# FFN tile pairs as seven half-size products: every other one from the seventh tile on

## What is computed

```python
def conv_ffn(h, w_up, conv_w, conv_b, w_down):
    up = h @ w_up                                    # 1024 -> 2 * 2816
    gate = causal_dwconv(up[..., :FFN_HIDDEN], conv_w, conv_b)   # 3 taps over tokens
    val = up[..., FFN_HIDDEN:]
    return (jax.nn.silu(gate) * val) @ w_down

for i in range(DEPTH):
    ...
    x = x + rms_norm(m, mix_post_g[i])
    f = conv_ffn(rms_norm(x, ffn_pre_g[i]), ffn_w_up[i], ffn_conv_w[i], ffn_conv_b[i], ffn_w_down[i])
    x = x + rms_norm(f, ffn_post_g[i])
```

## Time and profile before

| | us |
|---|---|
| median of three runs | 1339.46 (1339.46 to 1339.63) |
| profiled execution: own time | 1340.12 |
| profiled execution: span | 1338.4 |
| TensorE busy | 1327.8 (99%) |
| VectorE busy | 786.2 (59%) |
| ScalarE busy | 570.9 (43%) |
| chain that ended last: share of TensorE | 98% |

### The profile page before, as it was taken

How to read it: one execution, slowest core, us unless ns; L and a number is a source line. 1 busy time by engine, 2 the same in 40 slices (tenths; PEclk the granted TensorE clock), 3 DMA queues, 4 the chain that set the end, 5 groups by cost and what they waited for, 6 DMA issues and landing times.

```text
span 1338.4 us, 15750 instructions
## 1 busy us (share of the span) xinstructions
PE 1327.8 (99%) x6382; PEld 1109.5 (83%) x6382; DVE 786.2 (59%) x1140; ACT 570.9 (43%) x875; POOL 28.1 (2%) x30
## 2 busy tenths in 40 slices
PE   8999999999999999999999999999999999999998
PEld 6888888888888888888888888888888888888886
DVE  5888888888526666556632265445566666564223
ACT  6766665556315533333331262223554333333112
POOL 1000000000000000000000000000000000000000
PEclk9999999999999999999999999999999999999999
DMA  5533233442331333333343313334233333334331
GB/s 155 158 110 110 80 97 109 125 121 69 128 108 48 95 107 98 95 95 95 95 137 115 95 32 112 102 102 126 63 88 102 95 97 101 102 96 126 97 109 63
DMA packets 181772, 135.68 MB, mean 101 GB/s; under 512 B 5645, under 2 KB 169893, under 8 KB 180677
## 3 DMA queue, kind: packets, MB, share of 16 engines
q1 hardware_dynamic: 181653, 134.62, 33.5%
q10 hardware_dynamic: 48, 0.07, 0.0%
HBM read 132.51 MB, written 2.16 MB: 101 GB/s over the span
## 4 chain that ended last, share of the span: by engine, by line
PE 98%; ACT 1%; DMA 1%; DVE 0%; issue 0%; SPq 0%; DVEq 0%; ACTq 0%
PE bank L863 22%; PE bank L864 22%; PE bank L865 22%; PE bank L926 9%; PE bank L928 9%; PE bank L927 9%; PE bank L1065 1%; PE bank L1075 1%; PE bank L903 1%; PE bank L1055 1%; DMA x_tok<-in_x 1%; PE bank L1048 1%; PE bank L1040 0%; PE bank L1043 0%; PE bank L1001 0%; ACT mask L423 0%
## 5 line engine op out<-in xcount | busy, mean ns | idle before, releaser
L863 PE MATMUL bank<-h_hi,w_hi 128*128 128x512 f32 (+1 forms) x1328 | 509.0, 383 | 0.0
L865 PE MATMUL bank<-h_lo,w_hi 128*128 128x512 f32 (+1 forms) x1328 | 506.7, 382 | 0.0
L864 PE MATMUL bank<-h_hi,w_lo 128*128 128x512 f32 (+1 forms) x1328 | 506.5, 381 | 0.0
L592 DVE TENSOR_TENSOR w_lo<-w_raw,w_hi 128x1024 fp32r<-128x1024 f32 x227 | 285.1, 1258 | 324.2 <-ACT w_hi L362 324.2
L362 ACT ACTIVATE w_hi<-w_raw 128x1024 fp32r<-128x1024 f32 x227 | 237.1, 1051 | 196.3 <-PE bank L928 172.5
L865 PEld LDWEIGHTS bank<-h_lo,w_hi 128*128 128x128 f32 x1328 | 249.5, 188 | 48.2
L863 PEld LDWEIGHTS bank<-h_hi,w_hi 128*128 128x128 f32 x1328 | 249.6, 188 | 48.0
L864 PEld LDWEIGHTS bank<-h_hi,w_lo 128*128 128x128 f32 x1328 | 249.7, 188 | 47.6
L926 PE MATMUL bank<-w_hi,hid_hi 128*128 128x512 f32 x416 | 162.4, 390 | 0.0
L928 PE MATMUL bank<-w_hi,hid_lo 128*128 128x512 f32 x416 | 161.9, 389 | 0.0
L927 PE MATMUL bank<-w_lo,hid_hi 128*128 128x512 f32 x416 | 161.8, 389 | 0.0
(11 more groups left out here) (145 smaller groups left out, 941.7 us busy)
## 6 DMA issues: line engine op xcount, KB each, us to landing
w_raw<-in_ffn_w_up SPq DMA_DIRECT2D x88, 512.0 KB, 3.8
w_raw<-in_ssd_w_in SPq DMA_DIRECT2D x48, 512.0 KB, 3.9
w_raw<-in_ffn_w_down SPq DMA_DIRECT2D x44, 512.0 KB, 3.5
w_raw<-in_sc_w_in SPq DMA_DIRECT2D x24, 512.0 KB, 3.7
acs_b<-acs_dram SPq DMA_DIRECT2D x8, 1024.0 KB, 6.2
w_raw<-in_ssd_w_out SPq DMA_DIRECT2D x16, 512.0 KB, 3.5
w_raw<-in_sc_w_out SPq DMA_DIRECT2D x8, 512.0 KB, 3.6
x_tok<-in_x SPq DMA_DIRECT2D x4, 512.0 KB, 5.4
```

Of the source, the lines that this page charges most:

```text
L592: nc.vector.tensor_tensor(w_lo[slot(u)][:], w_raw[:, u % 2, :], w_hi[slot(u)][:].bitcast(F32), ALU.subtract).then_inc(w_lo_done, 1)
L863: nc.tensor.matmul(dst, wh, xh, start=start, stop=False)
L864: nc.tensor.matmul(dst, wl, xh, start=False, stop=False)
L865: return nc.tensor.matmul(dst, wh, xl, start=False, stop=stop)
```

## The change

In each layer the FFN tiles 0 to 5 stay plain. From tile 6 on, tiles 6, 8, ... 20 (eight per layer, `FAST`) are **pairs**, computed by the Winograd form of Strassen's scheme; tiles 7, 9, ... 21 stay plain (**singles**). For a pair, the gate and val units are the two rows of a 2 x 2 block matrix A whose columns are the halves of the inner 1024. The tokens' halves and the inner halves give B. Four sums of weights (`weight_sums`: S1, S3, S2, S4) and four sums of B (`block_sums`, once per layer) feed seven products (`up_pair`, `block`), each 4 inner tiles x 3 matmuls of 256 columns. Two of them run on top of an earlier product in the same bank. ScalarE copies three results out (`p1`, `p7`, `p6`), and VectorE makes five sums of 256 columns (`early`, `side`'s halves, `pu`, `late`).

Around it:
- High and low parts are now made of A11 A12, S3 S2, S4 A22 and S1 (`aa_`, `ss_`, `sa_`, `s1_` with `high` on ScalarE and `low` on VectorE): three of 1024 elements and one of 512 per pair, in four slots of the same five. `s_two` and `s_one` hold sums.
- Pairs have two raw buffers of their own, `w_raw_b`. A pair's loads wait for `sa_low` of the pair before.
- `hid` keeps float32 hidden tiles, and the norm row is no longer multiplied into val; the post norm gets a changed epsilon instead (`q_up`, one 128x4 operation on ScalarE at the boundaries before the FFNs). `side`'s multiply is gone from plain tiles: `gate_single` reads the bank.
- Hidden high and low parts are made in the down projection, tiles k + 2 ahead, in a ring of ten (`hs_hi`, `hs_lo`; `hid_high`, `hid_low`). Until the last pair is done, eight of the ten places hold the sums of B.
- `project` now waits ahead of token tile 0 for the last pair's sums, and ahead of tile 3 for all 22 hidden tiles (`hid_taken`).

The core of the diff (`aa_low` stands for its three likes; ScalarE's halves mirror it with the copies, each behind a wait for its slot):

```diff
+    PLAIN = 6
+    FP = (FT - PLAIN) // 2
+    FAST = [U_UP[layer] + 2 * (PLAIN + 2 * i) + half for layer in range(DEPTH) for i in range(FP) for half in range(2)]
...
+    READ = {"A11 A12": 2, "S3 S2": 4, "S4 A22": 6, "S1": 7}
...
+            n = FAST.index(u) // 2
+            for part, read in READ.items():
+                USE[n, part] = len(FREED)
+                FREED.append((True, PRODUCTS * n + read))
...
+        else:
+            RAW_FREED.append((True, FAST.index(u) // 2) if u in FAST else (False, nth(older[-1])))
...
-                sp.dma_start(dst.rearrange(view, n=P) if view else dst, src).then_inc(raw_landed[u % 2], 16)
+                if RAW_FREED[u] is not None:
+                    of_pairs, count = RAW_FREED[u]
+                    sp.wait_ge(sa_lo_done if of_pairs else w_lo_done, count)
...
+                for i in range(FP):
+                    n, t, more = FP * layer + i, PLAIN + 2 * i, i + 1 < FP
+                    single = gate_of(n) + 2
+                    split_at[0] = single
+                    act.wait_ge(prod_done, PRODUCTS * n + 1)
+                    if n:
+                        act.wait_ge(summed_up, SUMS * n)
+                    nc.scalar.copy(p1[:], bank[pair_bank(layer, AT_P1)][:, 0:HALF_T]).then_inc(copied, 1)
+                    splits_to(single + 1)
+                    act.wait_ge(prod_done, PRODUCTS * n + 3)
+                    nc.scalar.copy(p7[:], bank[pair_bank(layer, AT_P7)][:, 0:HALF_T]).then_inc(copied, 1)
+                    splits_to(single + 2)
+                    act.wait_ge(prod_done, PRODUCTS * n + 4)
+                    nc.scalar.copy(p6[:], bank[pair_bank(layer, AT_P1)][:, 0:HALF_T]).then_inc(copied, 1)
+                    if more:
+                        aa_high(layer, i + 1)
+                        ss_high(layer, i + 1)
+                        sa_high(layer, i + 1)
+                    else:
+                        splits_to(single + 4)
...
+            def aa_low(layer, i):
+                n, u = FP * layer + i, gate_of(FP * layer + i)
+                at = slot((n, "A11 A12"))
+                dve.wait_ge(aa_hi_done, n + 1)
+                nc.vector.tensor_tensor(w_lo[at][:], raw(u), w_hi[at][:].bitcast(F32), ALU.subtract).then_inc(aa_lo_done, 1)
...
+                dve.wait_ge(copied, COPIES * n + COPY_P6)
+                dve.wait_ge(prod_done, PRODUCTS * (n + 1))
+                nc.vector.tensor_tensor(pu[:], p6[:], bank[pair_bank(layer, AT_P5)][:, 0:HALF_T], ALU.add).then_inc(summed_up, 1)
+                dve.wait_ge(summed_up, SUMS * n + SUM_U)
+                nc.vector.tensor_tensor(late, pu[:], bank[pair_bank(layer, AT_P3)][:, 0:HALF_T], ALU.add).then_inc(summed_up, 1)
+                dve.wait_ge(summed_up, SUMS * n + SUM_C12)
+                whole = cpad[:, CW - 1:CW - 1 + T]
+                nc.vector.tensor_tensor(whole, whole, r_row[:, 0, :], ALU.mult).then_inc(gate_in, 1)
+                nc.vector.tensor_tensor(side[:, HALF_T:], pu[:], p7[:], ALU.add).then_inc(summed_up, 1)
...
+                    whole(b12, 0, 1)
+                elif part == 1:
+                    dve.wait_ge(t_made, at + 2)
+                    nc.vector.tensor_tensor(b11, b12, b11, ALU.subtract).then_inc(t_made, 1)
+                    whole(b22, 1, 1)
+                elif part == 2:
+                    dve.wait_ge(t_made, at + 4)
+                    nc.vector.tensor_tensor(b12, b22, b12, ALU.subtract).then_inc(t_made, 1)
...
+                dve.wait_ge(raw_landed[RAW_PLACE[u]], RAW_COUNT[u])
+                dve.wait_ge(raw_landed[RAW_PLACE[u + 1]], RAW_COUNT[u + 1])
+                if n:
+                    dve.wait_ge(s1_lo_done, n)
+                    dve.wait_ge(ss_lo_done, n)
+                nc.vector.tensor_tensor(s_one[:], a21, a22, ALU.add).then_inc(s_made, 1)
+                nc.vector.tensor_tensor(s3, a11, a21, ALU.subtract).then_inc(s_made, 1)
+                dve.wait_ge(s_made, 4 * n + 1)
+                nc.vector.tensor_tensor(s2, s_one[:], a11, ALU.subtract).then_inc(s_made, 1)
+                dve.wait_ge(s_made, 4 * n + 3)
+                nc.vector.tensor_tensor(a21, a12, s2, ALU.subtract).then_inc(s_made, 1)
...
+                dve.wait_ge(unit_done, nth(u))
+                if n:
+                    dve.wait_ge(tap_done, 2 * n)
+                nc.vector.tensor_tensor(cpad[:, CW - 1:CW - 1 + T], bank[UP_BANKS[layer][2 * (t % 2)]][:], r_row[:, 0, :],
+                                        ALU.mult).then_inc(gate_in, 1)
...
+            def gate_single(layer, t):
+                dve.wait_ge(unit_done, nth(U_UP[layer] + 2 * t + 1))
+                dve.wait_ge(act_done, FT * layer + t + 1)
+                nc.vector.tensor_tensor(hid[:, t, :], bank[UP_BANKS[layer][2 * (t % 2) + 1]][:], acc[:], ALU.mult).then_inc(gated_done, 1)
...
+                for t in range(PLAIN):
+                    u, end = U_UP[layer] + 2 * t, gate_of(FP * layer)
+                    gate_row(layer, t)
+                    splits_to(min(u + 4, end))
+                    if t in (1, 2):
+                        block_sums(layer, 2 * t - 2)
+                    elif t == 3:
+                        t_low(layer, 0)
+                        t_low(layer, 1)
+                    elif t == 4:
+                        weight_sums(layer, 0)
+                    elif t == 5:
+                        ss_low(layer, 0)
+                    gate_taps(layer, t)
+                    splits_to(min(u + 5, end))
+                    if t in (1, 2):
+                        block_sums(layer, 2 * t - 1)
+                    elif t == 3:
+                        t_low(layer, 2)
+                        t_low(layer, 3)
+                    elif t == 4:
+                        aa_low(layer, 0)
+                    elif t == 5:
+                        sa_low(layer, 0)
...
+                    gate_single(layer, t)
+                hid_at[0] = 0
+                for i in range(FP):
+                    n, t, more = FP * layer + i, PLAIN + 2 * i, i + 1 < FP
+                    single = gate_of(n) + 2
+                    split_at[0] = single
+                    splits_to(single + 1)
+                    dve.wait_ge(copied, COPIES * n + COPY_P1)
+                    dve.wait_ge(prod_done, PRODUCTS * n + 2)
+                    dve.wait_ge(tap_done, 2 * (HID0[2 * layer] + t))
+                    nc.vector.tensor_tensor(early, p1[:], bank[pair_bank(layer, AT_P2)][:, 0:HALF_T], ALU.add).then_inc(summed_up, 1)
+                    splits_to(single + 2)
+                    if more:
+                        weight_sums(layer, i + 1)
+                        aa_low(layer, i + 1)
+                    else:
+                        splits_to(single + 3)
+                        hid_low(layer, FIRST)
+                    dve.wait_ge(copied, COPIES * n + COPY_P6)
+                    dve.wait_ge(prod_done, PRODUCTS * n + 6)
+                    if i:
+                        dve.wait_ge(gated_done, HID0[2 * layer] + t - 1)
+                    nc.vector.tensor_tensor(side[:, 0:HALF_T], p6[:], bank[pair_bank(layer, AT_P7)][:, 0:HALF_T],
+                                            ALU.add).then_inc(summed_up, 1)
+                    last_sums(layer, i)
+                    if more:
+                        ss_low(layer, i + 1)
+                    else:
+                        splits_to(single + 4)
+                    gate_taps(layer, t)
+                    if more:
+                        sa_low(layer, i + 1)
+                    gate_pair(layer, t)
+                    gate_row(layer, t + 1)
+                    if more:
+                        s1_low(layer, i + 1)
+                    gate_taps(layer, t + 1)
+                    gate_single(layer, t + 1)
+                for k in range(2, FT):
+                    splits_to(U_DOWN[layer] + k + 1)
+                    hid_low(layer, k + 2)
             def sc_in(i):
                 u, n = U_SC + 3 * i, HID0[1] + i
...
+                for k in range(KT // 2):
+                    cols = slice(late * HALF_D + k * P, late * HALF_D + (k + 1) * P)
+                    last = three(dst, w_hi[at][:, cols], w_lo[at][:, cols], x_hi[:, k, :], x_lo[:, k, :],
+                                 start and k == 0, stop and k == KT // 2 - 1, skip_group_check=not start)
...
+            def up_pair(layer, i):
+                n = FP * layer + i
+                t_hi, t_lo = ([t_part(hs, k) for k in range(4)] for hs in (hs_hi, hs_lo))
+                pe.wait_ge(aa_lo_done, n + 1)
+                if n:
+                    pe.wait_ge(summed_up, SUMS * n)
+                block(layer, i, "A11 A12", 0, AT_P1, quarter(h_hi, 0, 0), quarter(h_lo, 0, 0), True, True)
+                block(layer, i, "A11 A12", 1, AT_P2, quarter(h_hi, 1, 0), quarter(h_lo, 1, 0), True, True)
+                pe.wait_ge(ss_lo_done, n + 1)
+                if i == 0:
+                    pe.wait_ge(t_lo_done, 4 * layer + 2)
```

(65 more changed lines are left out.)

289 lines of the change are left out of this document (207 added, 82 removed).

## The result

The changed kernel takes 1327.27 us (median, 1327.05 to 1327.39) against 1339.55 us before (1339.46 to 1339.68): ratio 0.9907, with a 95% interval of 0.9895 to 0.9920. It is 12.3 us faster; 12.8 were forecast. The profiled execution took 1327.05 us, its span 1325.3.

What follows compares the result with a forecast made beforehand. TensorE's matmul stream was taken as the bound: 16 pairs at 0.80 us save 12.8 from 1340.12, giving 1327.3, and the median's 0.66 offset gives 1326.6 us; other terms cost 0. Range 1325.4 to 1331.0 us.

Steps and rivals of the forecast that it cites:

- TensorE as the bound, and its step as the price: Whole kernel: time is TensorE's matmuls times their step, 0.2267 us at 512 columns and 0.1200 at 256.
- The ceilings given for these: Product seams in pairs: taken as 0, at most 0.07 us each, 7.8 us in all; reopened banks 0 to 0.07.
- The 12.8 us: TensorE's gain in the FFN pairs: 10.88 to 10.08 us a pair, 0.80 saved in each of 16.
- VectorE's loop: Pair and single: without TensorE the VectorE and ScalarE order would turn in 17.9 us, under TensorE's 20.96.
- The step rule: VectorE operations: step 0.08 us under the duration when the next doesn't wait for it, 0.03 over when it does.
- The stage's first tiles: Plain FFN tiles: added block sums and low parts make 9.8 us on VectorE, under TensorE's 10.88; cost 0.
- the hand-over: After the last pair, into the down projection: sums and hidden tiles ready before needed; cost 0, upper bound 1 us a layer.
- Loads: Pair's two raw weight transfers, waiting for sa_low: two landings 7.6 us, there at 24.1, wanted at 27.8; cost 0.
- C: Rival: steps in the pairs follow the skill's formula, fixed part 0.0025 us, gain 19 us, 1320.5 us; chance 0.03.
- B: Rival: product seams or the hand-over loop take part of the gain, 1327.6 to 1334 us; chance 0.14.
- D: Rival: the loop of pair loads binds, 22.25 us a period with two longest landings, 1342.1 us; chance 0.05.
- E: Rival: VectorE's loop takes about 21.7 us, 0.8 over TensorE, and eats the gain, 1339 us; chance 0.03.

Runs made afterwards that it cites:

- the trace of the loop alone: Changed kernel with the pairs' products cut to high by high matmuls, all VectorE and ScalarE work kept, output not exact: 1272.16 us, ratio 0.9499.

## Why the prediction was right

- TensorE as the bound, and its step as the price: right. 0.1200 us held for all 84 matmuls of a pair, with sums as weights, with reopened banks and with a wait at each product. The ceilings given for these (0.07 us a seam, up to 7.8 us) were not touched. The experiments with more and with narrower matmuls put the same prices on the other side, 13.4 us and, in the stages, 16.2.
- The 12.8 us: 12.5 in the two stages. The term that was mis-sized is the single beside a pair: 10.91 instead of 10.88 us, since the first wide matmuls behind narrow ones start 0.01 us further apart, 0.3 us in all. The rest of the distance from 1326.6 to 1327.27 us, about 0.4, is of the size by which the time ahead of the first FFN stage moves from run to run; no run shows its cause.
- VectorE's loop: 17.9 forecast, 17.82 measured; slack 3.0 against 3.2. The step rule, 0.08 under a duration or 0.03 over it by whether the next waits, carried this. The Trainium skill, "VectorE: DVE Perf Modes", section "The DRAIN you can't avoid", says that the next operation does not start until the pipe is empty; worked out by that sentence the loop was 20.0 us, an estimate, and the trace of the loop alone, 17.82, disagrees with it. The same section also says that an operation that is not held starts earlier, which the prediction left out and with which the steps of 0.08 under a duration agree.
- The stage's first tiles, the moved hidden splits, the hand-over and q_up at nothing: right; the 313.98 us between the stages are the same to the hundredth.
- Loads: of two that go together, each takes 5.2 us to land as the median, and they are issued 0.5 us apart, where I had added 3.8 and 3.8. The room was about 2 us larger than I wrote, and the conclusion the same.
- Rivals: C would have given 1320.5, by a fixed part of 0.0025 us; both widths and both experiments speak for 0.0133. The section "Back-to-back issue gap" of "TensorE: Matmul & The Clock Gate" in the Trainium skill gives that formula for the gap of an isolated matmul, and the prediction applied it to a stream. B, D and E did not happen. D and E could be brought about, with 8.5 us more delay of the loads and with 5.0 us more work on VectorE; 5.1 and 2.2 us did nothing.

## What to carry to other kernels

Where TensorE runs without a gap, price a smarter algorithm by the number of matmuls times their measured step at the new width, not by its multiplications: an eighth fewer columns became 7.2% of a pair's time (0.78 of 10.88 us), as shorter matmuls pay the fixed part more often. Then write out one period of the other engines' fixed order with steps from the trace, and look for the loop that goes through several engines; its length against TensorE's period tells how much work can be added for nothing, and the first wait on TensorE that fails, not the largest room, tells what it costs beyond.

## What was not expected of the hardware

A wide matmul that follows narrow ones starts its successor late: 0.23 to 0.24 us for the first few against 0.2267, about 0.02 us in all at each change from 256 to 512 columns. The other way nothing is lost (the first step is 0.11, 495.83 to the next at 495.94), nor between equal widths (a period of 21.60 us is 180 steps of 0.1200). And two matmuls in a row with the same weights save nothing: steps of 0.12 us in either order.
